# A seven-product scheme on half-size blocks for the projection's chunks 19 to 44

## The reference

```python
def project(x, g_norm, w_in):
    h = rmsnorm(x, g_norm)
    z = h @ w_in
    offs = [int(o) for o in np.cumsum(SPLITS)[:-1]]
    return jnp.split(z, offs, axis=-1)
# q, k, v, gate_a, qi, ki, wi, u, gate_s, qm, gate_m = project(x, g_norm, w_in)
# score = sum over 16 index heads of wi * relu(qi . ki); _, idx = lax.top_k(score, 256)
# s5_branch: xr, xi = u @ B; h = associative_scan(a, x); y = Re(C h) + D u; gelu; glu
# mix = concat(o_a * silu(gate_a), o_s * silu(gate_s), o_m * silu(gate_m)); y = x + mix @ w_out
```

## Time and profile before

| | us |
|---|---|
| device time, median of 3 runs | 1860.49 |
| lowest and highest | 1860.46, 1860.87 |
| profiled execution, first to last instruction | 1859.2 |

### The profile page before, as it was taken

How to read it: one execution, slowest core, us unless ns; L and a number is a source line. 1 busy time by engine, 2 the same in 40 slices (tenths; PEclk the granted TensorE clock), 3 DMA queues, 4 the chain that set the end, 5 groups by cost and what they waited for, 6 DMA issues and landing times. The chain is left out here.

```text
span 1859.2 us, 30880 instructions
## 1 busy us (share of the span) xinstructions
PE 1779.6 (96%) x12569; PEld 1210.3 (65%) x12569; DVE 1017.3 (55%) x1951; ACT 832.5 (45%) x1399; POOL 302.8 (16%) x217
## 2 busy tenths in 40 slices
PE   6999999999999999999999996998999899999997
PEld 4565555556666666666666664774554488888886
DVE  6564136547978687686868440554543752221226
ACT  5554557664344344333434321654443863333331
POOL 3022210111111121121212111026202300000000
PEclk9999999999999999999999998999999899999999
DMA  9522121112222322322232207503223722222224
GB/s 359 156 91 69 56 64 47 58 47 81 77 70 81 81 77 81 81 77 69 81 82 77 85 24 283 192 7 79 59 74 106 274 70 70 93 71 69 75 88 188
DMA packets 192289, 179.83 MB, mean 97 GB/s; under 512 B 30674, under 2 KB 171634, under 8 KB 189522
## 3 DMA queue, kind: packets, MB, share of 16 engines
q1 hardware_dynamic: 171938, 137.15, 24.0%
q10 hardware_dynamic: 14640, 22.96, 3.4%
q0 software_dynamic: 5568, 17.72, 2.8%
HBM read 143.59 MB, written 34.20 MB: 96 GB/s over the span
## 5 line engine op out<-in xcount | busy, mean ns | idle before, releaser
L703 PE MATMUL ps<-h,w 128*128 128x352 f16 (+2 forms) x6096 | 943.7, 315 | 1.6 <-PEq L223 1.0
L703 PEld LDWEIGHTS ps<-h,w 128*128 128x128 f16 (+1 forms) x6096 | 595.2, 99 | 333.4 <-issue 16.8
L987 POOL TENSOR_TENSOR w<-wb,w 128x2048 f16<-128x2048 f32 x44 | 184.0, 4182 | 812.1 <-ACT w L834 812.1
L2463 PE MATMUL ps<-w_f,m 128*128 128x256 f16 x2688 | 295.8, 273 | 4.4 <-DVE y_room L2538 2.9
L2463 PEld LDWEIGHTS ps<-w_f,m 128*128 128x128 f16 x2688 | 262.3, 98 | 36.6 <-issue 6.4
L1204 DVE MAX8 m<-score 128x8 f32<-128x1024 f32 (+2 forms) x192 | 171.6, 893 | 5.7
L1205 DVE MATCH_REPLACE8 score<-m,score 128x1024 f32<-128x1024 f32 (+2 forms) x192 | 168.1, 875 | 0.0
L842 ACT ACTIVATE zst<-ps,unit 128x352 f32<-128x352 f32 (+1 forms) x88 | 49.8, 582 | 252.1 <-PE ps L703 228.6
L2553 DVE SCALAR_TENSOR_TENSOR y_room<-ps,unit_f,x_f 128x256 f32<-128x256 f32 (+1 forms) x64 | 30.8, 483 | 219.5 <-PE ps L2463 189.6
L1196 DVE SCALAR_TENSOR_TENSOR score<-room,wis,score 128x1024 f32<-128x1024 f32 (+5 forms) x90 | 92.7, 1030 | 78.5 <-ACT room L904 73.0
L830 ACT ACTIVATE wb<-wb,unit 128x2048 f32<-128x2048 f32 x44 | 88.1, 2003 | 89.9 <-DVE unit L1004 89.9
(11 more groups left out here) (477 smaller groups left out, 1818.1 us busy)
## 6 DMA issues: line engine op xcount, KB each, us to landing
wb<-in_w_in_dram SPq DMA_DIRECT2D x44, 1024.0 KB, 5.0
z_scratch<-zst ACTq DMA_DIRECT2D x32, 528.0 KB, 2.7
score<-in_w_out_dram SPq DMA_DIRECT2D x7, 2048.0 KB, 11.6
y_room<-z_scratch SPq DMA_DIRECT2D x8, 1056.0 KB, 18.0
x_in<-in_x_prompt_dram SPq DMA_DIRECT2D x8, 1024.0 KB, 8.8
w_kv<-in_w_mem_kv_dram POOLq DMA_DIRECT2D x16, 512.0 KB, 6.9
x_f<-in_x_prompt_dram SPq DMA_DIRECT2D x8, 1024.0 KB, 5.2
out_y_p_dram<-y_room SPq DMA_DIRECT2D x7, 1024.0 KB, 3.9
```

The lines of the kernel that those rows point to most:

```text
L703: last = nc.tensor.matmul(ps[0:m, n, 0:w], w16[:, b, pw_, k, 0:m], h16[:, ph, k, t0:t0 + w], start=(k == 0 and i == 0), stop=(k == KT - 1 ...
L987: nc.gpsimd.tensor_tensor(w16[:, b, 1, :, 0:w], wb[:, b, :, 0:w], w16[:, b, 0, :, 0:w], ALU.subtract).then_inc(w_split, 1)
L2463: last = nc.tensor.matmul(ps[:, bank(b, i), 0:SLAB], m16[:, mp, k, t * P:(t + 1) * P], weights(s, b, wp, k), start=(k == 0 and j == 0), st ...
```

## The change

Chunks 0 to 18 stay. Chunks 19 to 44 become 13 slabs (`N_S`) of two chunks, c and c + 1. A slab is a 2 x 2 arrangement of weight blocks, each 8 k-tiles by 128 columns: a11 and a12 are the two halves over k of chunk c, a21 and a22 those of chunk c + 1. On the second and the last third of the tokens the four blocks are multiplied by a scheme of seven products (P1 to P7) on sums of blocks and sums of tokens; the first third is multiplied as before (R1a, R1b, R2a, R2b). That is 11 products of 24 matmuls, 264 a slab where two chunks had 288.

* Sums of tokens, a third wide, are made once, and kept on chip in f16 halves: `make_sums` (GpSimd, 5 operations for each of 8 k-tiles), `high_sums` (ScalarE) and `low_sums` (VectorE, 3 operations) beside chunks 15 to 18, and the last ones in slab 0, over the last third of h16's early k-tiles: `make_last` and `low_last` (VectorE, 4 operations for each of 8 k-tiles) and `high_last` (ScalarE).
* Sums of weight blocks, s1 to s4, are f32 operations of 128x1024 on GpSimd (`sum_operand`). Each slab has eight operands, whose high halves are ScalarE's and low halves GpSimd's, in a ring of four places of `w16`.
* Two products add up in one PSUM bank where the scheme allows it; the other combinations are VectorE's (`combine`: C22, C11, C21, each a product in PSUM times the unit, added to what `zst` holds). Gate slabs then take a silu on ScalarE (`finish`).
* One unit serves a slab (`set_slab_unit`). Its sum matmul (`sum_slab`) stands behind P3 of the slab before and waits for C11 of that slab, whose bank it shares.
* Loads come in quarters of 512 KB. `score` gives room to the operands: the scores go to DRAM at chunk 17 (`s_dram`), the tiles are ranked one after another, widest first, and SP brings each in and takes it out; `block_c` loads the whole.
* Ranking is dealt out by columns: `RANK_BEFORE` for chunks 15 to 18, `RANK_FIRST` ahead of C22, `RANK_SECOND` ahead of C11 and behind the unit, by x.
* The gelu's output now lies in `u_in`'s room, so `pad`, which sets zeros there for the next batch at x = 6, waits for all 24 stores of y; these are issued in parts along ScalarE's slab (`store_y`).

```diff
--- before.py
+++ after.py
...
+SCORED_AT = 17
+SUMS_AT = 15
+RANK_BEFORE = [0, 3000, 0, 3000]
+RANK_FIRST = [7200, 7200, 2600, 7200, 7200, 1700, 6400]
+RANK_SECOND = [(2200, 3900), (2200, 3900), (0, 1300), (2200, 3900), (2200, 3900), (0, 900), (1800, 3400)]
...
+OPERANDS = ("a11", "s2", "s3", "s1", "a12", "s4", "a21", "a22")
+GROUPS_DONE = ("P1", "R1a", "P6", "P7", "P5", "R1b", "P2", "P3", "R2a", "R2b", "P4")
+LAST_USE = dict(a11="R1a", s2="P6", s3="P7", s1="P5", a12="P2", s4="P3", a21="R2a", a22="P4")
+ACT_READS = ("E1", "E6", "H", "R1", "C12", "R2")
...
-        kw_f = sb("kw_f", [P, 2 * PER * MV])
-        y_out = kw_f[:].rearrange("p (a i n) -> p a i n", a=2, i=PER)
+        u_flat = room[:, 0:2 * PER * COLS]
+        y_out = u_flat[:, 0:2 * PER * MV].rearrange("p (a i n) -> p a i n", a=2, i=PER)
...
+            for i in range(N_S):
+                if i + 1 < N_S:
+                    sp.wait_ge(w_split, operand(i, "s1"))
+                    load_quarter(i + 1, 0)
+                    sp.wait_ge(s_made, summed(i, "s4"))
+                    sp.wait_ge(w_split, operand(i, "a12"))
+                    load_quarter(i + 1, 1)
+                    sp.wait_ge(w_split, operand(i, "s4"))
+                    sp.wait_ge(w_summed, sized(i + 1, 0))
+                    load_quarter(i + 1, 2)
+                    sp.wait_ge(w_split, operand(i, "a21"))
+                    sp.wait_ge(w_summed, sized(i + 1, 1))
+                    load_quarter(i + 1, 3)
+...
+            def slab(i):
+
+                first = i == 0
+                pe.wait_ge(w_split, operand(i, "a11"))
+                pe.wait_ge(z_evac, before(FIRST_S - 1) + 1 if first else read(i - 1, "C12"))
+                product(i, "P1", "a11", 0, early(H1), True, True)
+                if not first:
+                    pe.wait_ge(z_evac, read(i - 1, "R2"))
+                product(i, "R1a", "a11", 7, early(0), True, False)
+
+                pe.wait_ge(w_split, operand(i, "s2"))
+                pe.wait_ge(z_evac, read(i, "E1"))
+                if first:
+                    pe.wait_ge(t_low, t_low_0 + LATE_K)
+                product(i, "P6", "s2", 0, turned_sum(2), False, True)
+
+                pe.wait_ge(w_split, operand(i, "s3"))
+                if first:
+                    pe.wait_ge(z_evac, before(FIRST_S - 1) + 2)
+                else:
+                    pe.wait_ge(added, add(i - 1, "C21"))
+                product(i, "P7", "s3", 1, turned_sum(1), True, True)
+
+                pe.wait_ge(w_split, operand(i, "s1"))
+                pe.wait_ge(z_evac, read(i, "E6"))
+                product(i, "P5", "s1", 0, turned_sum(0), False, True)
+                states(FIRST_S + 2 * i)
+
+                pe.wait_ge(w_split, operand(i, "a12"))
+                product(i, "R1b", "a12", 7, later(0), False, True)
+                if first:
+                    pe.wait_ge(z_evac, before(FIRST_S))
+                else:
+                    pe.wait_ge(added, add(i - 1, "C11"))
+                product(i, "P2", "a12", 2, later(H1), True, True)
+
+                pe.wait_ge(w_split, operand(i, "s4"))
+                pe.wait_ge(z_evac, read(i, "H"))
+                product(i, "P3", "s4", 0, later(H2), False, True)
+
+                pe.wait_ge(w_split, operand(i, "a21"))
+                pe.wait_ge(z_evac, read(i, "R1"))
+                if i + 1 < N_S:
+                    sum_slab(i + 1)
+                product(i, "R2a", "a21", 7, early(0), True, False)
+
+                pe.wait_ge(w_split, operand(i, "a22"))
+                product(i, "R2b", "a22", 7, later(0), False, True)
+                pe.wait_ge(added, add(i, "C22"))
+                if first:
+                    pe.wait_ge(t_low, t_low_0 + 2 * LATE_K)
+                product(i, "P4", "a22", 1, early(H2), False, True)
+                states(FIRST_S + 2 * i + 1)
...
+            def high_last(k):
+
+                act.wait_ge(t_made, t_made_0 + LATE_K + k + 1)
+                if k == 0:
+                    act.wait_ge(z_ready, before(FIRST_S))
+                src = sums_a[:, k % 3 * WIDTH:(k % 3 + 1) * WIDTH]
+                nc.scalar.activation(h16[:, 0, k, H2:H2 + WIDTH], src, ACT.Copy).then_inc(t_high, 1)
...
+            for i in range(N_S):
+                c = FIRST_S + 2 * i
+                scale(i, "a12")
+                high(i, "s2")
+                high(i, "s3")
+                if i:
+                    finish(i - 1, "C21")
+                    store_slab(i - 1, 1)
+                act.wait_ge(z_stored[0], 16 * stores(c))
+                evac_slab(i, "E1")
+                if i == 0:
+                    for k in range(4):
+                        high_last(k)
+                state_copy(c)
+                gelu(c)
+                high(i, "s1")
+                if i == 0:
+                    for k in range(4, LATE_K):
+                        high_last(k)
+                high(i, "a12")
+                store_y(c, 0, 4)
+                act.wait_ge(z_stored[1], 16 * stores(c + 1))
+                evac_slab(i, "E6")
+                high(i, "s4")
+                store_y(c, 4, 8)
+                high(i, "a21")
+                if i + 1 < N_S:
+                    sum_quarter(i + 1, 0)
+                store_y(c, 8, 12)
+                evac_slab(i, "H")
+                high(i, "a22")
+                state_copy(c + 1)
+                gelu(c + 1)
+                if i + 1 < N_S:
+                    sum_quarter(i + 1, 1)
+                evac_slab(i, "R1")
+                store_y(c + 1, 0, 4)
+                if i + 1 < N_S:
+                    sum_quarter(i + 1, 2)
+                    sum_quarter(i + 1, 3)
+                store_y(c, 12, Y_DMAS)
+                store_y(c + 1, 4, 8)
+                evac_slab(i, "C12")
+                finish(i, "C11")
+                store_slab(i, 0)
+                if i + 1 < N_S:
+                    start_slab(i + 1)
+                store_y(c + 1, 8, 14)
...
+            for k in range(2 * (FIRST_S - 1 - SUMS_AT), LATE_K):
+                make_sums(k)
+            for i in range(N_S):
+                low(i, "a11")
+                pool.wait_ge(w_split, operand(i, "a11"))
+                pool.wait_ge(act_link, scaled(i, "a21"))
+                sum_operand(i, "s3", "a11", "a21", ALU.subtract)
+                pool.wait_ge(s_made, summed(i, "s3"))
+                pool.wait_ge(act_link, scaled(i, "a22"))
+                sum_operand(i, "s2", "a22", "s3", ALU.subtract)
+                low(i, "s2")
+                low(i, "s3")
+                pool.wait_ge(w_split, operand(i, "s3"))
+                sum_operand(i, "s1", "a21", "a22", ALU.add)
+                low(i, "s1")
+                pool.wait_ge(act_link, scaled(i, "a12"))
+                sum_operand(i, "s4", "a12", "s2", ALU.subtract)
+                low(i, "a12")
+                low(i, "s4")
+                low(i, "a21")
...
+            def pad(c):
+
+                t, x = turn(c)
+                if x == 6 and t + 1 < BATCHES:
+                    dve.wait_ge(y_stored, 16 * Y_DMAS * (t + 1))
+                    memset(u_in[SPAN * GROUP // 2:, :, 0:DEC_BATCH], 0.0)
+                    memset(u_in[0:SPAN * GROUP // 2, :, DEC_BATCH + BLKS:COLS], 0.0).then_inc(padded, 1)
...
+            def make_last(k):
+
+                out = sums_a[:, k % 3 * WIDTH:(k % 3 + 1) * WIDTH]
+                link(TT(out, h16[:, 0, LATE_K + k, H1:H1 + WIDTH], h16[:, 1, LATE_K + k, H1:H1 + WIDTH], ALU.add))
+                link(TT(out, out, t_half(k, 2, 0), ALU.subtract))
+                TT(out, out, t_half(k, 2, 1), ALU.subtract).then_inc(t_made, 1)
+
+            def low_last(k):
+
+                dve.wait_ge(t_high, t_high_0 + LATE_K + k + 1)
+                TT(h16[:, 1, k, H2:TOK], sums_a[:, k % 3 * WIDTH:(k % 3 + 1) * WIDTH], h16[:, 0, k, H2:TOK],
+                   ALU.subtract).then_inc(t_low, 1)
...
+            for c in range(START, FIRST_S):
+                if c + 1 < FIRST_S:
+                    set_unit(c + 1)
+                work = of_states(c)
+                advance(work, 3)
+                if c >= SUMS_AT:
+                    low_sums(2 * (c - SUMS_AT))
+                advance(work, 2)
+                if c >= SUMS_AT:
+                    low_sums(2 * (c - SUMS_AT) + 1)
+                advance(work)
+                rank(budget())
+            set_slab_unit(0)
+            for i in range(N_S):
+                c = FIRST_S + 2 * i
+                if i:
+                    combine(i - 1, "C21")
+                else:
+                    for k in range(LATE_K):
+                        make_last(k)
+                        if k:
+                            low_last(k - 1)
+                    low_last(LATE_K - 1)
+                work = of_states(c)
+                advance(work)
+                rank(budget())
+                combine(i, "C22")
+                work = of_states(c + 1)
+                advance(work, 3)
+                rank(budget())
```

(8 more changed lines are left out.)

484 lines of the change are left out of this document (414 added, 70 removed).

## The result

| | before | after |
|---|---|---|
| device time, median, us | 1860.47 (4 runs) | 1895.03 (4 runs, 1891.42 to 1900.27) |
| profiled execution, first to last instruction | 1859.2 | 1889.7 (its device time: 1891.42) |
| chunk 19 begins; last projection matmul ends | 526.6; 1124.8 | 537.2; 1157.3 |

The ratio is 1.0192, with a 95% interval from 1.0175 to 1.0209: slower by 1.9%. The forecast was 1898, with a range of 1849 to 1918. The profile is of the fastest of the four runs, 3.6 us under the median.

The account below looks back on a forecast made before the run. TensorE bound the kernel before; in the slabs VectorE was to be level with it. TensorE's 56.5 us less and 94.4 us of lateness gave +37.9 on 1859.2, plus 1.3: 1898 us, range 1849 to 1918.

Parts of the forecast that it names:

- TensorE's part: From chunk 19 to the last projection matmul, TensorE's work without waits takes 541.7 us, 56.5 us less than before.
- A: Entry to slab 0: P1 starts late after chunk 18, behind token sums, ranking rounds and the unit; 22 us (9.4 to 28).
- B: Slab 0: make_last and low_last take turns with GpSimd, so R1b waits for a12; 16 us (9 to 20).
- C: Slab 1: pad waits for the y stores, as in E but delaying less; 4.7 us (2.7 to 7).
- E: Slab 4: pad waits for all 24 y stores, making C11 and the unit late; 16.8 us (13.6 to 19).
- F: Slab 6: run_states ahead of C22, its 14 long two-SBUF operations waiting for GpSimd; 14.5 us (0 to 20).
- other slabs: Slabs 2, 7, 8, 9 and 11: VectorE's own work exceeds TensorE's; 15.7 us (10 to 20).
- slow clock: TensorE's clock is half after long waits, four or five of them; 4 us (2 to 8).
- tail: End of the loop: C21 and its silu stand behind P4; 0.7 us.
- TensorE, feed, port: TensorE's work 541.7 us; GpSimd 26.3 and ScalarE 23 of 39.5 us a slab; two-SBUF operations wait for GpSimd's current one.
- rival 4: GpSimd's f32 addition takes 3.06 us, so a12 is late by about 1 us per slab: 1911; 0.57 together with the forecast.
- (1): Rival: TensorE stays the bound and the port lock costs next to nothing, A + B + F under 25 us: 1850; chance 0.20.

Follow-up runs that it names:

- e2: Changed kernel with GpSimd making only one eighth of each low half of a slab's operands, so not a whole kernel: 1873.1 us, ratio 1.0068.
- e9: Changed kernel with chunk 16's three ranking rounds ahead of its token sums instead of behind them: 1890.3 us, ratio 1.0164.
- e6: Changed kernel with P6 of slab 0 evacuated by ScalarE ahead of the last four high halves of the token sums: 1892.6 us, ratio 1.0174.
- e1: Changed kernel with pad moved behind C11 and the next slab's unit, in every slab: 1897.6 us, ratio 1.0209.
- e11: e10 with ranking rounds dealt out by slab, fewer ahead of C11 in slabs 1, 5, 8 and 10, more in slab 11: 1834.2 us, ratio 0.9864.
- e3: Changed kernel with the edits of e1 and e2 together, so not a whole kernel: 1859.7 us, ratio 0.9993.
- e8: Changed kernel, pad late, slabs 4 and 6's early rounds in slab 12, make(0) first, P6 evacuated early, chunk 18's rounds in slab 0: 1856.6 us, ratio 0.9992.
- e10: e8 with the edit of e9 added: 1849.5 us, ratio 0.9943.
- e4: Changed kernel with the next slab's sum matmul waiting for C22 instead of C11, and the unit set ahead of C11's rounds: 1917.5 us, ratio 1.0317.

## Why the prediction was right, step by step

The time, the sign and the mechanism held: TensorE does less and waits more, since VectorE and ScalarE, with GpSimd on the shared port, come late where TensorE needs them. The sum is better than its terms. They stand here beside what the trace shows:

| step | taken | measured |
|---|---|---|
| TensorE's part | 541.7 | 541.7 stands as the base; 35.0 us less busy in all, slow clock included |
| A, entry | 22 | 17.3 |
| chunk 19's start late | no term | 10.6 |
| B, slab 0 | 16 | 12.9 |
| C, slab 1 | 4.7 | 2.8 |
| E, slab 4 | 16.8 | 12.5 |
| F, slab 6 | 14.5 | 12.7 |
| other slabs | 15.7 | 6.7 (2.5 + 3.7 + 0.5) |
| slow clock | 4 | 13.5 (what is left of 89.0) |
| tail | 0.7 | not seen apart |

* **TensorE, feed, port.** These steps held. GpSimd's times were within 5% of those by size; rival 4 fell, with sums of 2.4 us. The port took turns as the rows had shown, and e2 puts its price in slab 6 at 10.9 us of the 12.7. The Trainium skill's rule of an exclusive lock (SBUF — State Buffer, "Who interferes with whom") agrees with this trace, where the product of 0.75 us took 2.69 and 2.91. The 115 ns that the prediction weighed are what the same page gives in "A bandwidth-pool intuition that's wrong" for descriptors that wait for VectorE; no run here tells such an addition apart.
* **A** was inside its bounds and 4.7 us too dear at the value taken, and it was not all of the entry. The chain was rightly told (e9 took 6.5 us from it by one of its members), but TensorE also waits for 9.9 us in chunk 15, for `make(0)`, before it can make kernels. The prediction had `make(0)` only as a sharer of the port, not as something that TensorE waits for: this term is missing.
* **B** had the price within 3 us and the wrong wait. It had R1b wait for a12, behind the token sums on the port, and ScalarE's queue delay only what comes later. In the trace P5 waits for the evacuation of P6, behind the late high halves on ScalarE, and that order made 10.2 of the 12.9 us (e6). With it gone, TensorE waits for weights: 2.8 us at P5 for s1, and 2.7 us at R1b for a12, the wait that B had named.
* **C** was a small wait with another cause: it stays without pad (2.74 us in e1), and goes where fewer rounds stand ahead of C11 (e11).
* **E** had the price and the arithmetic of the stores (36 forecast, 33.5 measured), but took the chain for the only one. `make` in the same slab got the port's price too, and alone would have given nearly the same wait (e1, e3).
* **F** was near in size. Its 14 long two-SBUF operations are 10, since four of the twelve products read PSUM, as the last line of the earlier trace rows has it.
* **The other slabs** were too dear by 9 us. The ledger charged each slab its own surplus, in slabs 2, 7, 8, 9 and 11; the trace has waits in 8 and 10 alone. That a slab with slack takes in what the one before left is a reading that fits, and was not tried by itself.
* **Slow clock** was too cheap by 9.5 us: I had it for the long waits only. The 13.5 us are a remainder, but the granted clock of the stretch, summed over windows of 2 us, gives 12.4 us lost.

The other slabs and slow clock nearly cancel, 9.0 too dear and 9.5 too cheap. The missing 10.6 us of the entry make up for most of the 15.8 by which A, B, C, E and F were too dear. That the sum is 5.4 us off in the profile, and 3 us in the median, is in part luck.

Of the signs that the prediction named, TensorE's idle time over 50 us (64.9), the products over 2 us in slab 6 and GpSimd's 27 us a slab came as told. P1 came 17.3 us after chunk 18, between the 22 forecast and the 9 that would refute the lock, and slab 4's wait was 12.5 us, not 15 or more.

Of the rivals, (1) had the right bound: it decides at some 25 us for A + B + F. By their waits, the one for `make(0)` included, e8 has 25 there and stands level with the kernel before, e10 has 18 and is faster. Its condition, a port that costs next to nothing, is not what these runs have: they leave GpSimd's work as it was and change the order.

## What to carry to other kernels

Where a change makes a second engine as full as the first, count who waits for whom within each stage, not only the sums: here 312 matmuls fewer, 46.6 us, came with 60 us more of waits (64.9 for 5.3) in that stretch, and moving the same work (ranking rounds, pad, `make(0)`, one evacuation) to where nothing waits for it gave 61 us back. If a wait has two chains that end together, a profile names one; take away each and both before believing it. An edit that makes one thing early tests nothing if another engine still waits for what comes behind it, as ScalarE did in e4. An edit that frees 10 us at one place should be read at the end of the stage, since what follows can absorb it.
